# Inverting the chunk matrices of an RWKV-7 recurrence in 32x32 blocks instead of 64x64, and one low part moved to GpSimd

## What is computed

```python
def rwkv_step(S, inp):
    r_t, w_t, k_t, v_t, a_t, b_t = inp
    sa = jnp.einsum('bhij,bhj->bhi', S, a_t)
    S = S * w_t[:, :, None, :] + sa[..., None] * b_t[:, :, None, :] + v_t[..., None] * k_t[:, :, None, :]
    return S, jnp.einsum('bhij,bhj->bhi', S, r_t)
...
    S_fin, y = lax.scan(rwkv_step, S0.astype(F32), (tm(r), tm(decay), tm(k), tm(v), tm(-kk), tm(kk * a)))
    y = tm(y)
    y = head_norm(y, P['rwkv_lnx_g'][e].reshape(H_B, DH_B), P['rwkv_lnx_b'][e].reshape(H_B, DH_B), eps=LNX_EPS)
    y = y + jnp.sum(r * k * P['rwkv_rk'][e], axis=-1, keepdims=True) * v
```

## Time and profile before

| | |
|---|---|
| median of 3 runs | 1446.66 us (1446.42 to 1448.36) |
| profiled execution: span from its first to its last instruction | 1443.7 us |
| median of the runs less that span | 3.0 us |
| TensorE busy | 1394.8 us (97%), 11496 products |
| VectorE, ScalarE, GpSimd busy | 1056.3 us, 349.0 us, 353.3 us |
| mean granted TensorE clock | 0.979 of 2.4 GHz |

### The profile page before, as it was taken

How to read it: one execution, slowest core, us unless ns; L and a number is a source line. 1 busy time by engine, 2 the same in 40 slices (tenths; PEclk the granted TensorE clock), 3 DMA queues, 4 the chain that set the end, 5 groups by cost and what they waited for, 6 DMA issues and landing times.

```text
span 1443.7 us, 28382 instructions
## 1 busy us (share of the span) xinstructions
PE 1394.8 (97%) x11496; PEld 1287.2 (89%) x11496; DVE 1056.3 (73%) x1366; ACT 349.0 (24%) x670; POOL 353.3 (24%) x300
## 2 busy tenths in 40 slices
PE   9999999999988998999999999999999999999997
PEld 9999999996343987999999999999996679999996
DVE  6977676768977546798768598769578687887764
ACT  5111102002453434511111311110202455211100
POOL 0533212005400023453311253311200002533310
PEclk9999999999998989999999999999999989999998
DMA  8443542664787104544346344345161305444152
GB/s 324 163 157 117 193 165 92 213 226 169 270 292 288 53 3 179 215 158 174 116 167 211 130 164 173 118 159 199 65 221 77 152 34 226 175 150 170 52 171 80
DMA packets 63194, 233.27 MB, mean 162 GB/s; under 512 B 9019, under 2 KB 18816, under 8 KB 46204
## 3 DMA queue, kind: packets, MB, share of 16 engines
q1 hardware_dynamic: 50970, 224.82, 43.3%
q10 hardware_dynamic: 11554, 6.37, 1.5%
q0 software_dynamic: 576, 0.74, 0.2%
HBM read 225.67 MB, written 6.10 MB: 161 GB/s over the span
## 4 chain that ended last, share of the span: by engine, by line
PE 49%; DVE 5%; POOL 3%; ACT 2%; issue 1%; DMA 0%; POOLq 0%; DVEq 0%; ACTq 0%
PE psum L193 15%; PE psum L195 15%; PE psum L194 15%; DVE x L421 1%; DVE hidden_hi L417 1%; DVE rstd L316 1%; POOL hidden L331 0%; POOL hidden L333 0%; PE psum L377 0%; POOL ysq_ab_out L3086 0%; DVE x_lo_r L310 0%; PE psum L374 0%; DMA ring<-in_w_cd 0%; POOL sq_ab_out L331 0%; POOL sq_cd_out L331 0%
## 5 line engine op out<-in xcount | busy, mean ns | idle before, releaser
L193 PE MATMUL psum<-x_hi_r,pair_hi 128*128 128x288 f32 x1736 | 515.7, 297 | 4.6 <-PEq L123 2.2
L195 PE MATMUL psum<-x_hi_r,ring_r 128*128 128x288 f32 x1736 | 514.5, 296 | 0.0
L194 PE MATMUL psum<-x_lo_r,pair_hi 128*128 128x288 f32 x1608 | 474.8, 295 | 0.0
L188 DVE TENSOR_TENSOR ring_r<-ring,pair_hi 128x2048 fp32r<-128x2048 f32 (+1 forms) x129 | 335.8, 2605 | 26.2 <-ACT pair_hi L183 22.4
L193 PEld LDWEIGHTS psum<-x_hi_r,pair_hi 128*128 128x128 f32 x1736 | 328.2, 189 | 7.3 <-issue 5.8
L195 PEld LDWEIGHTS psum<-x_hi_r,ring_r 128*128 128x128 f32 x1736 | 327.6, 189 | 0.0
L194 PEld LDWEIGHTS psum<-x_lo_r,pair_hi 128*128 128x128 f32 x1608 | 303.4, 189 | 0.3
L193 PE MATMUL psum<-hidden_hi_r,down_hi 128*128 128x288 f32 x704 | 208.4, 296 | 0.0
L194 PE MATMUL psum<-hidden_r,down_hi 128*128 128x288 f32 x704 | 207.7, 295 | 0.0
L195 PE MATMUL psum<-hidden_hi_r,down_r 128*128 128x288 f32 x704 | 207.0, 294 | 0.0
L732 POOL TENSOR_TENSOR hidden<-silu,up 128x288 f32 x88 | 125.7, 1428 | 144.5 <-ACT silu L652 142.6
(11 more groups left out here) (562 smaller groups left out, 1852.7 us busy)
## 6 DMA issues: line engine op xcount, KB each, us to landing
ring<-in_w_gu SPq DMA_DIRECT2D x87, 1024.0 KB, 4.8
down<-in_w_down SPq DMA_DIRECT2D x64, 704.0 KB, 4.3
ring<-in_w_ab SPq DMA_DIRECT2D x18, 1024.0 KB, 5.2
ring<-in_w_cd SPq DMA_DIRECT2D x12, 1024.0 KB, 5.6
ring<-in_cache_k SPq DMA_DIRECT2D x32, 256.0 KB, 4.3
index_keys<-in_cache_k SPq DMA_DIRECT2D x32, 256.0 KB, 5.4
index_keys<-in_cache_i ACTq DMA_DIRECT2D x64, 64.0 KB, 2.8
eight_pages_ds<-in_cache_v SPq DMA_DIRECT2D x16, 256.0 KB, 6.1
```

Of the source, the lines that this page charges most:

```text
L188: return eng.tensor_tensor(lo, a, hi.bitcast(F32), ALU.subtract)
L193: pe.matmul(out, w_hi, x_hi, start=start, stop=False)
L194: pe.matmul(out, w_hi, x_lo, start=False, stop=False)
L195: return pe.matmul(out, w_lo, x_hi, start=False, stop=stop)
```

## The change

The matrices are taken apart into blocks of 32. The two diagonal blocks of each of the 40 matrices are inverted by themselves, each in a quadrant of the array of its own (`QUADS`: rows and columns 32 to 63 and so on), in four squaring rounds (A^32 is 0 for a block of 32), with the running inverse `XQ` started from the product of A with the identity. The block beside the diagonal is then made by two products: `EDGE` = A's edge block times one inverse, and the other inverse, transposed as `LEFT`, times that. The sample chunk has only 32 tokens and needs neither. X is put together from shares: ScalarE writes one half of the columns, GpSimd the other, and VectorE adds the edge block. The key-value products of the chunks are spread between the rounds. The low part of the first pair of output weights, which VectorE took after round 3, is taken by GpSimd (`first_low_part`), ahead of its share of X and of the restricted keys.

```diff
+QB = 32
+QUADS = tuple((q, b, slice(q * L + b * QB, q * L + b * QB + QB)) for q in range(2) for b in range(2))
...
+    def first_low_part(pool):
+
+        slot = out.first % RING
+        pool.wait_ge(c.pair_masked, out.first + 1)
+        low_bits(pool, c.ring_lo[:, slot], c.ring[:, slot], c.whi[:, slot]).then_inc(c.pair_split, 1)
+
     def restricted_keys(pool):
 
-        pool.wait_ge(S["x_out"], N_POWERS)
+        pool.wait_ge(S["x_out"], X_MADE - 2)
+        pool.tensor_tensor(X[:, :, QB:L], XQ, bc(last_rows.rearrange("p (m a) -> p m a", m=1), [P, CH * HP, QB]), ALU.mult).then_inc(S["x_shares"], 1)
+        pool.wait_ge(S["x_out"], X_MADE)
...
-        dve.wait_ge(S["dve_out"], 15)
-        for q in range(2):
-            for c_ in range(CH):
-                last = dve.tensor_tensor(X[half(q), c_ * HP:c_ * HP + HP], G[half(q), c_, q, :, 0:L],
-                                         bc(id2[half(q), :].rearrange("p (a n) -> p a n", a=1), [64, HP, L]), ALU.add)
-        last.then_inc(S["x_out"], 1)
...
+        for k_ in range(5):
+            for g, (m0, m1) in enumerate(GROUPS[k_ > 1]):
                 n += 1
                 dve.wait_ge(S["x_sum"], n)
-                w = (m1 - m0) * L
-                dve.tensor_tensor(X[:, m0:m1], X[:, m0:m1], B[6 + n % 2][:, 0:w].rearrange("p (m n) -> p m n", n=L), ALU.add).then_inc(S["x_out"], 1)
-            if it == 2:
+                old = XQ[:, m0:m1] if k_ else bc(quad_id.rearrange("p (m l) -> p m l", m=1), [P, m1 - m0, QB])
+                dve.tensor_tensor(XQ[:, m0:m1], narrow(4 + g, m1 - m0), old, ALU.add).then_inc(S["x_out"], 1)
+            if k_ == 2:
                 dve.wait_ge(A["kv_used"], NB + 5)
                 dve.wait_ge(c.ring_landed[out.first % RING], 16 * (out.first // RING + 1))
                 mask(dve, c.whi[:, out.first % RING], c.ring[:, out.first % RING]).then_inc(c.pair_masked, 1)
-            if it == 3:
-                dve.wait_ge(c.pair_masked, out.first + 1)
-                low_bits(dve, c.ring_lo[:, out.first % RING], c.ring[:, out.first % RING], c.whi[:, out.first % RING]).then_inc(c.pair_split, 1)
+        dve.wait_ge(S["edge_sum"], 1)
+        dve.tensor_copy(EDGE[:, :, :], narrow(3, 16)).then_inc(S["x_out"], 1)
+        dve.wait_ge(S["edge_sum"], 2)
+        dve.wait_ge(S["x_shares"], 2)
+        dve.scalar_tensor_tensor(X[:, 0:16, QB:L], narrow(4, 16), first_rows, X[:, 0:16, QB:L], ALU.mult, ALU.add).then_inc(S["x_out"], 1)
...
+        def blocks(bank, m0, m1, left, right, quads=QUADS):
+            for m in range(m0, m1):
+                for q, b, rows in quads:
+                    mm = pe.matmul(B[bank][rows, (m - m0) * QB:(m - m0) * QB + QB], left(m, q, b, rows), right(m, q, b, rows), start=True, stop=True)
+            return mm
+
+        pe.wait_ge(S["act_out"], CH)
+        key_values(0)
         pe.wait_ge(S["act_out"], 2 * CH)
...
+        for g, (m0, m1) in enumerate(GROUPS[0]):
+            pe.wait_ge(S["dve_out"], 12 + 3 * g)
+            blocks(g, m0, m1, upper, lower).then_inc(S["pw_sum"], 1)
+            blocks(2 + g, 8 * g, 8 * g + 8, lower, upper).then_inc(S["pwt_sum"], 1)
+            pe.wait_ge(S["dve_out"], 13 + 2 * g)
+            blocks(4 + g, m0, m1, lower, identity).then_inc(S["x_sum"], 1)
+        key_values(1)
+        for k_ in range(1, 5):
+            power = kept(POW[(k_ - 1) % 2])
+            for g, (m0, m1) in enumerate(GROUPS[1]):
+                n = 2 * (k_ - 1) + g + 1
                 pe.wait_ge(S["pw_out"], n)
...
+                if k_ < 4:
+                    pe.wait_ge(S["pwt_out"], n)
+                    blocks(g, m0, m1, kept(TPOW), power).then_inc(S["pw_sum"], 1)
+                    if k_ < 3:
+                        blocks(2 + g, m0, m1, power, kept(TPOW)).then_inc(S["pwt_sum"], 1)
+                pe.wait_ge(S["x_out"], n)
+                blocks(4 + g, m0, GROUPS[k_ > 1][g][1], power, kept(XQ)).then_inc(S["x_sum"], 1)
+            if k_ < 4:
+                key_values(1 + k_)
+
+        for g, (m0, m1) in enumerate(GROUPS[1]):
+            pe.wait_ge(S["x_out"], 9 + g)
+            for m in range(m0, m1):
+                for q in range(2):
+                    top, low = QUADS[2 * q][2], QUADS[2 * q + 1][2]
+                    pe.matmul(B[3][top, m * QB:m * QB + QB], LOW[low, m, 0:QB], XQ[low, m], start=True, stop=True)
+                    mm = pe.matmul(B[2][top, m * QB:m * QB + QB], XQ[top, m], quad_id[top], start=True, stop=True)
+        mm.then_inc(S["edge_sum"], 1)
...
-GROUPS = (((0, 8), (8, 16), (16, 20)), ((0, 8), (8, 16)))
-N_POWERS = 1 + len(GROUPS[0]) + 4 * len(GROUPS[1])
+GROUPS = (((0, 8), (8, 20)), ((0, 8), (8, 16)))
+X_MADE = 12
```

More of the change, by code:

```diff
@@ L871, in recurrence @@
     spare = idx.keys[:, :].rearrange("p b n -> p (b n)")
-    PW, PWT = ([spare[:, o:o + MATS].rearrange("p (m l) -> p m l", l=L) for o in os] for os in ((0, MATS), (2 * MATS, 3 * MATS)))
+    LOW = spare[:, 0:MATS].rearrange("p (m l) -> p m l", l=L)
+    POW = [spare[:, MATS + i * MATS // 2:MATS + (i + 1) * MATS // 2].rearrange("p (m l) -> p m l", l=QB) for i in range(2)]
+    TPOW, XQ = (spare[:, 2 * MATS + i * MATS // 2:2 * MATS + (i + 1) * MATS // 2].rearrange("p (m l) -> p m l", l=QB) for i in range(2))
+    LEFT, EDGE = (spare[:, 3 * MATS + i * 16 * QB:3 * MATS + (i + 1) * 16 * QB].rearrange("p (m l) -> p m l", l=QB) for i in range(2))
     U = spare[:, 4 * MATS:6 * MATS].rearrange("p (c q h l) -> p c q h l", c=CH, q=2, h=HP)
@@ L1172, in chunks @@
         sample_state(3)
+        dve.wait_ge(c.pair_split, out.first + 1)
         low_pair(c, dve, out.first, 1)
@@ L1377, in chunk_products, with key_values @@
             g += 1
-        pe.wait_ge(S["act_out"], CH)
-        for c_ in range(CH):
-            if c_ < 4:
-                pe.wait_ge(S["dve_out"], g - 3)
+        def key_values(c_):
+            if c_ < 2:
+                pe.wait_ge(S["dve_out"], 12 + 3 * c_)
             else:
-                pe.wait_ge(S["act_out"], 2 * CH + c_ - 3)
+                pe.wait_ge(S["act_out"], 2 * CH + c_ - 1)
             for h in range(HP):
@@ L1387, in chunk_products @@
                     o = half(1 - q)
-                    mm = pe.matmul(B[4 + g % 4][half(q), h * L:h * L + L], G[o, c_, q, h, 0:L], U[o, c_, q, h], start=True, stop=True)
+                    mm = pe.matmul(B[7 - c_ % 2][half(q), h * L:h * L + L], G[o, c_, q, h, 0:L], U[o, c_, q, h], start=True, stop=True)
             mm.then_inc(S["dve_grp"], 1)
-            g += 1
-        pe.wait_ge(S["act_out"], 2 * CH)
-        def transposed(src, m, q, it):
-            return G[half(q), m // HP, q, m % HP, 0:L] if it == 1 else PWT[src][half(q), m]
@@ L1434, in chunk_products, with lower, upper, identity @@
-        n_x = n
-        pe.wait_ge(S["prod_done"], HP)
-        for h in range(HP):
-            pe.matmul(B[h][:, 0:NT], c.half_ones[:, :], e2[:, h], start=True, stop=True).then_inc(S["kk_sum"], 1)
+        def lower(m, q, b, rows):
+            return LOW[rows, m, b * QB:b * QB + QB]
+        def upper(m, q, b, rows):
+            return G[rows, m // HP, q, m % HP, b * QB:b * QB + QB]
+        def identity(m, q, b, rows):
+            return quad_id[rows]
+        def kept(a):
+            return lambda m, q, b, rows: a[rows, m]
@@ L1439, in chunk_products, with bonus @@
+        def bonus(h):
+            pe.matmul(B[h][:, 0:NT], c.half_ones[:, :], e2[:, h], start=True, stop=True).then_inc(S["kk_sum"], 1)
+        pe.wait_ge(S["prod_done"], HP)
+        bonus(0)
+        bonus(1)
+        pe.wait_ge(S["pw_out"], 9)
+        pe.wait_ge(S["x_out"], X_MADE - 1)
+        blocks(4, 0, 16, kept(LEFT), kept(EDGE), QUADS[::2]).then_inc(S["edge_sum"], 1)
+        bonus(2)
+        bonus(3)
         pe.wait_ge(S["state_loaded"], 16)
@@ L3189, in lay_out_rwkv @@
     m["bmask"] = np.tile((s_ < NS) & (s_ // TS == np.arange(NB)[None]), (2, 1)).astype(np.float32)
-    m["id2"] = np.tile(np.eye(L, dtype=np.float32), (2, 1))
+    upper = (np.arange(P) // QB % 2 == 0).astype(np.float32)
+    m["quads"] = np.concatenate([np.tile(np.eye(QB, dtype=np.float32), (4, 1)), np.stack([upper, 1 - upper], 1)], 1)
 def lay_out_dsa(m, i):
```

81 lines of the change are left out of this document (25 added, 56 removed).

## The result

The changed kernel takes 1472.8 us, median of four runs (1468.31 to 1476.67), against 1446.85 us for the kernel before, run beside it (1446.42 to 1448.36): a ratio of 1.0176, 95% interval 1.0156 to 1.0196. The profiled execution spans 1474.9 us, 31.2 us more than the one of before; it is the longest of the four.

What follows compares the result with a forecast made beforehand. TensorE's rounds were taken as bound by TensorE, its instruction packets only just hidden. 1443.7 + 19.3 for more records, all else 0, made a span of 1463.0; 3.0 more for the median gave 1466 us, range 1444 to 1474 (0.8).

Steps and rivals of the forecast that it cites:

- likeliest case: The forecast's main case alone, instruction supply pacing the rounds: 1461 to 1473 us.
- What bounds the kernel now: Rounds, 31.3 us on TensorE: instruction packets, one fetched ahead, 3.4 us per 128 records, just hidden at 29.2 ns.
- Part 1, the supply: Rounds: 1904 records in place of 1024, at 3.4 us per 128: 50.6 us in place of 31.3, +19.3 us.
- the one packet that the ring load delays stays: In the rounds, the weight load's delay of one instruction packet, a stall of 1.04 us, was to stay.
- Part 2, no wait between rounds: Between rounds: a group takes TensorE 1.7 us, its move to SBUF shrinks to 0.38 us; nothing waits, 0.
- parts 3 and 4: Edge blocks: their moves lie beside products, 0; the ten VectorE additions of line 1084 (3.55 us) go, 0.
- Part 5, the low part: First low part, from VectorE to GpSimd: 5 us there, over long before the last power, 0.
- Part 6, the clock: Granted clock in the rounds and behind them: could fall to 1.2 GHz, 0 to +5.2 us; taken as 0.
- rival D: Rounds: the predicted supply limit with the clock down, 1471 us; chance 0.62 shared with the forecast and Rival C.
- Rival A: Rounds: no supply limit, tiles overlap at 9.2 ns a record: 21.5 us, -9.8, so 1437; chance 0.18.
- Rival C: Rounds: every record costs 29.2 ns whatever its size: 55.6 us, +24.3, 1471; chance 0.62 shared with the forecast, rival D.
- B and E: Rounds: sequencer alone, 14 to 17 ns, 1448 to 1453, chance 0.16; Rival A with clock down, 1450 to 1455, 0.04.

Runs made afterwards that it cites:

- experiment 6: First low part back on VectorE in the changed kernel (1476.90 us, ratio 1.0198); and, alone, moved to GpSimd in the kernel before (1449.36 us, 1.0012).
- e5_low_on_vector: Changed kernel with the first low part back on VectorE, behind the fourth round's sums: 1476.90 us, ratio 1.0198.
- e1_ring_late: Changed kernel with the first load of output weights issued after the last round and GpSimd's low part behind the restricted keys: 1472.14 us, ratio 1.0181.
- e10_merged: Changed kernel with three pairs of product sets made one, by products of 64 columns, 96 products fewer: 1472.59 us, ratio 1.0188.
- e13_before_joined: Kernel before with 368 round products in place of 472, those of rounds one to three joined to 128 columns: 1446.41 us, ratio 0.9991.
- e7_loop: Changed kernel with the four later rounds as a loop on TensorE, one power buffer and 128-column openers: 1469.09 us, ratio 1.0144.
- e9_loop_late: Changed kernel with the later rounds as a loop, openers of 8 columns, and the output weights' load issued after the rounds: 1472.63 us, ratio 1.0179.
- e12_before_more: Kernel before with eight extra 32x32 products ahead of each of its 31 sets of round products: 1461.38 us, ratio 1.0106.
- e8_before_loop: Kernel before with its 64x64 rounds two to five as a loop on TensorE, with 8-column openers: 1458.11 us, ratio 1.0065.

## Why the prediction was right

The direction, the cause and the order of size held; the time lies 6.8 us above the 1466, inside the likeliest case's range and the whole one, 0.2 and 1.2 us from their ends. That it still fell inside is in part luck: two terms were too small and one that was put at 0 wasn't, and 2.8 us of that came back elsewhere.

- *What bounds the kernel now* held. "Before, 29.2 ns hides it, just": the looped old rounds show 29 ns as TensorE's own pace with nothing to fetch, and a packet of such records lasts 3.74 us against the 3.4 to 3.8 that one takes to come.
- *Part 1, the supply*, held in kind: packets of 128 records, holes marked "issue", gone where nothing is fetched. Its size was too small: +25.75 us in place of +19.3. The mis-sized terms are two. 3.4 us is what a packet takes at best; from 493.66 to 542.81 us 13 intervals average 3.78 us, which over 14.9 packets makes 5.7 us more. And "the one packet that the ring load delays stays", at 1.04 us, was wrong: a delayed packet used to be covered by records that last 3.7 us and now by some that last 1.4, so the hole is 4.59 us, of which the late load gave back 2.2. The two terms make 9.2 us too little, and the sum was 6.5 too small: the 2.8 us between them go, as far as can be told, to the instructions already there at the start, for which the prediction took 1.04 us; no run measured them apart.
- *Part 2, no wait between rounds; parts 3 and 4*: held. No hole in the stretch ends with a semaphore.
- *Part 5, the low part*: 5 us taken, 4.50 measured, nothing on the path, shown by experiment 6.
- *Part 6, the clock, taken as 0*: failed. The granted clock fell to 0.50 at 491.8 us, in the first long hole, and stayed there to 543.0. The reason given, that four quadrants keep the array hardly ever without a moving column, doesn't hold: even the hole-free loop of small openers stayed at 0.50 for 22 us. What it cost is not in the stretch, as rival D also had it: with full products in the holes the packets came no faster. It is behind it, 13.6 us at half clock where before had 10.2 and 5.37 us for line 1474's records where before had 3.90: +1.6 us net in this execution. Two profiled executions with TensorE's code unchanged paid more or less there, against before: +4.7 us in e5_low_on_vector, +0.2 in e1_ring_late. So the range of the term, 0 to +5.2, was right and the value taken was not.
- *Rival A* (9.2 ns without a supply limit; its own row gives 9.0) was right about the array, 8.8 ns in the loop, and wrong about this kernel, which never gets its instructions that fast. *Rival D* (the supply with the clock down, 1471) is what happened, with a clock that cost less and packets that cost more than it had. *Rival C* gave 1471 too, by a mechanism that the loop excludes for 32x32: in the old rounds 29.2 ns a record can't be told from 3.75 us a packet. For products in the halves the floor is real: 8 columns cost 29 ns at full clock and (7.00 - 0.25) / 127 = 53 ns at half clock (e10_merged), so it goes with the clock and not with the supply. The Trainium skill's figure on that side ("TensorE: Matmul & The Clock Gate", Back-to-back issue gap, about 25 ns start to start) doesn't hold for products in separate quadrants, by the same 8.8 ns. The Trainium skill's sentence that instruction fetch is hidden ("Runtime: NRT & Kernel Launch", Instruction fetch mechanics) doesn't hold for products this small: 22.8 us of holes here.
- B and E need packets less than 3 us apart; none of the 15 intervals from 483.99 to 542.81 us is (3.4 to 5.8).

## What to carry to other kernels

Count instructions as well as columns: here 256 of TensorE's cost 3.4 to 3.8 us to bring, so a product that lasts under some 27 ns a record in straight code gains nothing by getting smaller, and splitting a matrix into four quadrants, which doubles the number of products, loses. If such small products are wanted, put them in a loop, whose body was fetched once here, and look at the granted clock; even so the loop tried here was still 22 us slower than the kernel before. Where the records of a stretch follow each other without a hole, at a pace that a fetch would give as well (29.2 ns against 3.75 us for 128), no arithmetic on that profile separates a floor per product from the fetch; a loop does.

## What the runs showed that I had not expected

Two rows of the kernel before help to read what a small product costs at full clock:

```profile
474.58 2.43 PE L1355 MATMUL psum<-ident,ring 128*128 128x128 f32 x20
...
1122.34 1.95 PE L2811 MATMUL psum<-qdec_cm,ring 64*128 64x4 f32 x32
```

- The two halves of the array do work side by side. Over the whole array records of 288 columns start (2.21 - 0.41) / 7 = 257 ns apart, 0.89 ns a column, and those of 128 columns (2.43 - 0.27) / 19 = 114 ns, the same per column. In alternating halves one of 128 columns starts every 55 ns (e13_before_joined), so two of them take the time of one.
- What a product of few columns doesn't get below goes with the columns of its weights in these rows: 4 columns on weights of 128 columns cost (1.95 - 0.25) / 31 = 55 ns, 8 columns on weights of 64 cost 29 ns, and 32 columns on weights of 32, in four quadrants, 8.8 ns (e7_loop; 13.3 ns at half clock, e9_loop_late). That is read from rows; no run changed the weights' columns alone.
- Sixteen records of 32x32 between products of 64x64 cost 0.41 us, where 16 x 8.8 ns make 0.14: the rest, 0.27 us, goes with the two changes of shape (e12_before_more).
- The clock stood at 1.2 GHz from 509 to 531 us of e9_loop_late, while TensorE was busy without a hole over 0.18 us with 32x32 products and 8-column openers; with openers of 128 columns it came back within the same loop 10 us earlier (521.3 against 531.7 us). In the loop of 64x64 products with 8-column openers (e8_before_loop) it never fell.
- The load of one megabyte stretched the interval between two packets to 5.26 us before and to 5.83 after the change; without it that interval was 3.71 us (e1_ring_late). The holes were 1.04 us, 4.59 and 2.40: what a late packet costs depends on how fast the instructions ahead of it run out.
